# The order in which 64 experts' weights are streamed: rank bits reversed, or largest and smallest in turn

## The chip, the cores and the metric

One core of a Trainium2 chip runs the whole program in one launch. The metric is device time in microseconds (us). The core has engines that run side by side and meet at semaphores: TensorE (PE, matrix products; PEld is its weight load), VectorE (DVE), ScalarE (ACT), GpSimd (POOL) and SyncE (SP), which here does nothing but issue DMAs and wait. Transfers from HBM run on 16 DMA engines that all queues share.

## The reference

Two transformer blocks over 512 tokens of width 1024, all in float32. The part that matters is the mixture of experts (MoE) of the first block: a router picks 8 of 64 experts for each token, and each chosen expert adds its result, weighted by a gate.

```
scores = sigmoid(h @ router_w);  e_idx = 8 best experts of each token (in 4 of 8 groups)
gate   = scores[e_idx] / sum * 2.5
expert e, for each of its tokens:  (silu(x @ w_gate[e]) * (x @ w_up[e])) @ w_down[e]
routed = sum over a token's 8 experts of gate * result;   shared expert added
```

`w_gate` and `w_up` are 1024 x 256 for each expert and `w_down` is 256 x 1024: 1 MiB each, 3 MiB an expert, 192 MiB in all. Which expert is worked on first makes no difference to the result: each of the 4096 (token, expert) results goes to a row of its own in HBM (`y_rows`), and is added up later.

## The kernel before, in words

**Tiles and turns.** An expert's tokens are cut into tiles of 64 rows (`HALF`); an expert has at least one tile, so a nearly empty one costs as much as a full tile. Two tiles make a turn: tile A (the even one) fills the upper half of the rows of TensorE's products, tile B (the odd one) the lower half, and both halves run at once, each with its own expert's weights. For tile A TensorE reads the weights where the DMA put them; for tile B VectorE first copies them (`copy_gu` at line 3223, `copy_down` at line 3234), since the two may be the same expert's.

**The order of a turn on TensorE** (lines 1478 to 1534): `turn_gu(n)` (lines 1493 and 1494: gate and up products), `turn_h(n-1)` (line 1502: transposes), `turn_rows(n+1)` (line 1480: transposes of the gathered tokens), `turn_down(n-1)` (lines 1514 and 1515), and on to `turn_gu(n+1)`. VectorE's order is `copy_gu(n)`, `turn_h(n-1)`, `copy_down(n-1)`, `copy_gu(n+1)`; there are two buffers for the copy of gate and up, so `copy_gu(n)` may begin once `turn_gu(n-2)` is done, and one for down. ScalarE does a tanh (line 2269) right after each `turn_gu`, and takes the result out of PSUM (line 2279) right after each `turn_down`. GpSimd gathers the tokens of coming turns by an indirect DMA and puts results away by another.

**The ring.** The weights of `RING = 4` experts are on the chip at a time. The experts are numbered by slot, 0 to 63, in the order in which they are loaded and worked on; slot k lies in place k mod 4. Slots 0 to 3 are always experts 0 to 3, since they are loaded before the router has spoken. The other 60 are ranked by their number of tokens on the chip, and `load_order()` says which rank (4 is the largest of the 60, 63 the smallest) goes to which slot: `counting_rows()` writes it into a constant, and line 3125 compares each expert's rank with it. Nothing is computed that depends on it but the table of slots, and with it tiles, turns and rows.

**The loads** are issued by SyncE in one fixed sequence, slot by slot (lines 744 to 757 and 789 to 799). For slot k:

```
wait until turn_gu and copy_gu are done with slot k-4       # ahead moe_g, moe_cg
issue w_gate, w_up of slot k                                # line 745
wait until gate and up of slot k-1 have landed; signal it   # landed_gu, line 752
wait until turn_down and copy_down are done with slot k-5   # ahead moe_y, moe_cd, in next_down
issue w_down of slot k-1                                    # line 748
wait until down of slot k-2 has landed; signal it           # landed_down, line 756
```

So the signal that gate and up of slot k-1 are there is given only behind the issue of slot k's gate and up, and that stands behind the issue of slot k-2's down. VectorE's `copy_gu` waits for the signal of its tile B's expert (`gu_loaded`), and TensorE's `turn_gu` waits for VectorE's copy, not for the signal itself. SyncE's waits on TensorE count whole turns: a slot whose last tile is tile t is let go when turn t // 2 is done.

**Idle turns.** The table is made for 128 tiles; the tiles that no expert needs stand at the front and are skipped four at a time.

Of the kernel before, what the change touches and what calls it, by code (L numbers as in the profile page):

```python
# [41 lines left out]
N_EXPERTS = 64  # L42
# [8 lines left out]
RING = 4  # L51
# [44 lines left out]

def load_order():

    pace = [r for r in (int(f"{n:06b}"[::-1], 2) for n in range(N_EXPERTS)) if r < N_EXPERTS - RING]
    return list(range(RING)) + [RING + r for r in pace]  # L100


def counting_rows():

    tokens = np.arange(P)[:, None] + P * np.arange(TT)[None, :]
    counts = np.broadcast_to(np.arange(P + 1)[None, :], (P, P + 1))
    pairs = (PER_TOKEN * tokens[:, :, None] + np.arange(PER_TOKEN)[None, None, :] + 1).reshape(P, -1)
    e = np.arange(P)
    prior = np.where(e < RING, (RING - e) * float(1 << 18), -e.astype(np.float64))
    order = np.concatenate([load_order(), np.zeros(P - N_EXPERTS)])  # L110
    experts = np.broadcast_to(e[None, :N_EXPERTS], (P, N_EXPERTS))
    return np.concatenate([tokens, counts, pairs, np.broadcast_to(prior[None, :N_EXPERTS], (P, N_EXPERTS)),
                           prior[:, None], order[:, None], experts], axis=1).astype(np.float32)
# [3539 lines left out]
```

How the kernel before makes its waits and increments, by code:

```python
    def wait(self):  # L220
        self.eng.wait_ge(self.sem, self.base + self.k)
# [439 lines left out]
        def ahead(eng, name, value):  # L661
            eng.wait_ge(sem(name), value + AHEAD[name])
# [25 lines left out]
        @block.sync  # L690
# [3 lines left out]
            def fill(name, u, turn, *parts):  # L694
                s = ring.slot(name, u)
                sp.wait_ge(used[s], ring.free(name, u, turn))
                for dst, src in parts:
                    sp.dma_start(dst, src).then_inc(landed[s], 16)
# [19 lines left out]
            with sp.Fori(0, 4) as i:  # L719
                for u in range(2):
                    fill("merge", 2 * u, i,
                         (unit("merge", 2 * u, 0, KD, P), w_in[:, :, bass.ds(i * 256 + (GA0 + u * P), P)]),
                         (unit("merge", 2 * u, 1024, KD, P), w_in[:, :, bass.ds(i * 256 + (GB0 + u * P), P)]),
                         (unit("merge", 2 * u, 2048, KD, P), w_sc_out[:, :, bass.ds(i * 256 + u * P, P)]))
                    fill("merge", 2 * u + 1, i,
                         (unit("merge", 2 * u + 1, 0, 16, P), w_ssd_out[:, :, bass.ds(i * 256 + u * P, P)]))
            for u in range(2):
                if u == 1:
                    sp.wait_ge(sem("ada_sum"), ADA_MERGE["sum"] + 8 * ADA_N - 1)
                fill("w_o", u, 0, (unit("w_o", u, 0, KD, 512), w_o[:, :, 512 * u:512 * u + 512]))
            sp.wait_ge(sem("ada_sum"), ADA_MERGE["sum"] + 8 * ADA_N)
# [17 lines left out]
            def landed_gu(slot, nth):  # L750
                sp.wait_ge(sem(f"ring_in{slot}"), nth * 32)
                sp.sem_inc(sem("gu_loaded"), 1)
```

## Time and profile before

| | us |
|---|---|
| three runs | 3205.16, 3205.81, 3209.31 |
| median | 3205.81 |
| the profiled execution | 3207.94 |
| its span | 3206.3 |
| TensorE busy | 3067.1 (96%) |
| VectorE busy | 1856.3 (58%) |
| the turns of the experts | about 1062 to 1704 |

The span is cut by the profile from the first to the last instruction; all positions below are us from its start. Over the whole span the 16 DMA engines move 177 GB/s on average; in the slices of the experts it is 364 to 392 GB/s. The busy time of TensorE overlaps the waits of its own pipeline, so it is not TensorE at its peak.

### The profile page before, as it was taken

Reading aid. Unit: us, or ns where it says so; the run is one execution under the profiler, and the core shown is the slowest. Engines: PE = TensorE matmul, PEld = TensorE weight load, DVE = VectorE, ACT = ScalarE, POOL = GpSimd, SP = SyncE. Lnnn points to the kernel's source line nnn. Section 1 sums busy time; section 2 is a strip of 40 time slices with the busy share of each in tenths; the row PEclk is TensorE's granted clock in tenths of the full one; section 3 lists DMA queues with packets and bytes.
Section 4 is the critical chain, followed back from the end, with each engine's and each line's share of the span. In section 5 each row is a group of like instructions: output and inputs, shape, how many; then the busy total and the mean of one; then the engine's idle time right before and its main releaser. Section 6 shows DMA issues by size and latency. Waiting matters only on the chain. (4 is left out here: it accounts for less than half of the span.)

```text
span 3206.3 us, 39693 instructions
## 1 busy us (share of the span) xinstructions
PE 3067.1 (96%) x12422; PEld 1759.3 (55%) x12423; DVE 1856.3 (58%) x3939; ACT 561.1 (18%) x1282; POOL 243.5 (8%) x377
## 2 busy tenths in 40 slices
PE   7999999999999899999997998999999899899998
PEld 4765666644447333333333445488744687488643
DVE  6767676565446534434334387565667555465667
ACT  1002222210002122222221216310000233100000
POOL 1000000011100222222212000000000000000000
PEclk9999999999999899999999999999999999899999
DMA  7673132388753479999997231022344324022342
GB/s 228 188 221 100 59 99 66 112 274 275 237 182 132 181 311 388 379 381 376 392 364 284 105 105 34 33 99 79 131 165 143 99 80 138 26 99 79 131 184 105
DMA packets 270691, 566.55 MB, mean 177 GB/s; under 512 B 27017, under 2 KB 162804, under 8 KB 245994
## 3 DMA queue, kind: packets, MB, share of 16 engines
q1 hardware_dynamic: 213712, 413.72, 36.2%
q0 software_dynamic: 46992, 140.43, 12.5%
q10 hardware_dynamic: 9866, 10.82, 1.0%
q8 instruction: 71, 1.16, 0.1%
q14 instruction: 50, 0.41, 0.0%
HBM read 554.22 MB, written 36.83 MB: 184 GB/s over the span
## 5 line engine op out<-in xcount | busy, mean ns | idle before, releaser
L1493 PE MATMUL ps<-WR,hT 128*64 x832 | 374.4, 604 | 20.7 <-issue 20.7
L1494 PE MATMUL ps<-WR,hT 128*64 128x512 f32 x832 | 374.4, 604 | 0.0
L1937 PE MATMUL ps<-WR 128*128 128x512 f32 x784 | 337.4, 592 | 1.0 <-DVEq L3511 0.7
L1493 PEld LDWEIGHTS ps<-WR,hT 128*64 128x64 f32 x832 | 115.5, 140 | 264.3 <-issue 264.2
L1937 PEld LDWEIGHTS ps<-WR 128*128 128x128 f32 x784 | 148.6, 190 | 188.9 <-issue 186.0
L3223 DVE COPY WR<-WR 128x1024 f32 x208 | 130.8, 691 | 161.8 <-SPq L752 108.6
L1157 PE MATMUL ps<-hT,WR 128*128 128x512 f32 x512 | 223.8, 593 | 0.6 <-DVE WR L2752 0.6
L1896 PE MATMUL ps<-WR 128*128 128x256 f32 x960 | 217.0, 379 | 0.0
L1896 PEld LDWEIGHTS ps<-WR 128*128 128x128 f32 x960 | 182.4, 190 | 24.8
L1514 PE MATMUL ps<-WR 128*64 x416 | 189.5, 598 | 2.7 <-DVEq L3236 1.8
L1515 PE MATMUL ps<-WR 128*64 128x512 f32 x416 | 189.6, 598 | 0.0
L1340 PE MATMUL ps<-WR 128*128 128x512 f32 x384 | 168.7, 598 | 1.5 <-ACT WR L2433 0.8
L3557 DVE TENSOR_TENSOR WR<-ps,WR 128x256 f32<-128x256 f32 x210 | 86.0, 423 | 145.1 <-PE ps L1896 143.3
L1896 PE MATMUL ps<-hT,WR 128*128 128x256 f32 x720 | 165.2, 379 | 0.0
L1157 PEld LDWEIGHTS ps<-hT,WR 128*128 128x128 f32 x512 | 96.5, 190 | 112.7 <-issue 111.0
L3234 DVE COPY WR<-WR 128x1024 f32 x104 | 67.3, 690 | 142.8 <-PE ps L1515 122.9
L1896 PEld LDWEIGHTS ps<-hT,WR 128*128 128x128 f32 x720 | 136.6, 190 | 18.5
L2581 DVE SCALAR_TENSOR_TENSOR WR<-xr,csil,WR 128x512 f32<-128x512 f32 x168 | 126.3, 752 | 11.7 <-DMA xr<-in_ada_w 3.3
L1340 PEld LDWEIGHTS ps<-WR 128*128 128x128 f32 x384 | 72.7, 192 | 91.0 <-issue 88.7
L1494 PEld LDWEIGHTS ps<-WR,hT 128*64 128x64 f32 x832 | 115.5, 140 | 0.0
L1173 PE MATMUL ps<-WR,hT 128*128 128x256 f32 x512 | 112.8, 379 | 0.0
L1234 PE MATMUL ps<-hT,WR 128*128 128x512 f32 x256 | 112.0, 594 | 0.0
(475 smaller groups left out, 4712.8 us busy)
## 6 DMA issues: line engine op xcount, KB each, us to landing
WR<-in_w_gate SPq DMA_DIRECT2D x64, 1024.0 KB
WR<-in_w_up SPq DMA_DIRECT2D x64, 1024.0 KB
WR<-in_w_down SPq DMA_DIRECT2D x64, 1024.0 KB
WR<-in_mlp_w SPq DMA_DIRECT2D x56, 1024.0 KB, 6.2
WR<-in_mlp_w SPq DMA_DIRECT2D x20, 2048.0 KB, 7.5
xr<-in_ada_w POOLq DMA_DIRECT2D x32, 1024.0 KB, 5.5
WR<-in_w_in SPq DMA_DIRECT2D x56, 512.0 KB, 6.9
xr<-in_w_ada POOLq DMA_DIRECT2D x16, 1024.0 KB, 5.4
```

The lines of the kernel that those rows point to most:

```text
L1157: last = mm(ps[:, k % 2, :], w[:, kk, k * P:(k + 1) * P], hT[:, kk, :], start=(kk == 0), stop=(kk == KD - 1))
L1173: last = mm(ps[:, h, (t % 2) * GW:(t % 2 + 1) * GW], hT[:, kk, t * P:(t + 1) * P], w[:, kk, :], start=(kk == 0), stop=(kk == KD - 1))
L1234: last = mm(ps[:, MERGE_BANKS[u][n], :], w[:, k, :], rhs[:, k, :], start=(k == 0), stop=(k == KD - 1))
L1340: last = mm(ps[:, 2 * t + u, :], src[:, k, t * P:(t + 1) * P], w[:, k, :], start=(k == 0), stop=(k == KD - 1))
L1493: mm(out[0:HALF], xT[u][:, k, 0:HALF], wa[:, :, k, :], start=(k == 0), stop=(k == KD - 1))
L1494: last = mm(out[HALF:P], xT[u][:, k, HALF:P], wb[:, :, k, :], start=(k == 0), stop=(k == KD - 1))
L1514: mm(ps[0:HALF, 5 + n, :], heT[u][:, f, 0:HALF], wa[:, f, n, :], start=(f == 0), stop=(f == FE - 1))
L1515: last = mm(ps[HALF:P, 5 + n, :], heT[u][:, f, HALF:P], wb[:, f, n, :], start=(f == 0), stop=(f == FE - 1))
L1896: last = mm(ps[:, bank, 0:2 * P], weights[:, k, :], tokens[:, k, :], start=(k == 0), stop=(k == 3))
L1937: return mm(ps[:, bank, :], rows, weights, start=(row == 0), stop=(row == PAST[phase] - 1))
L2581: ins = V.scalar_tensor_tensor(dst, w[:, k - lo, :], c[:, k:k + 1], dst, ALU.mult, ALU.add)
L3223: last = V.tensor_copy(gu_b[u][:, D * n:D * (n + 1)], w[:, D * n:D * (n + 1)])
```

## The change

One line of `load_order()`. Slots 0 to 3 stay. The 60 ranks that follow were in the order of their six bits reversed, with those of 60 and over left out; they now come as the first, the last, the second, the last but one and so on.

```diff
-    pace = [r for r in (int(f"{n:06b}"[::-1], 2) for n in range(N_EXPERTS)) if r < N_EXPERTS - RING]
+    pace = [r for n in range((N_EXPERTS - RING) // 2) for r in (n, N_EXPERTS - RING - 1 - n)]
     return list(range(RING)) + [RING + r for r in pace]
```

Both lists hold each of 0 to 59 once. The router of the reference, run on the inputs, gives these token counts: experts 0 to 3 have 20, 49, 91 and 16 tokens, the largest of the others has 332, then 184, 183, 180, 164, 151, 136 and 129, and so on down to 2. That makes 102 tiles: one expert with 6, seven with 3, nineteen with 2 (expert 2 among them) and thirty-seven with 1. By slot, beginning with slot 0, the tiles are

```
before  1 1 2 1 | 6 1 2 1 2 1 2 1 3 1 2 1 2 1 1 3 1 2 1 2 1 1 1 3 1 2 1 2 1 1
                  3 1 2 1 2 1 2 1 3 1 2 1 2 1 1 3 1 2 1 2 1 1 1 3 1 2 1 2 1 1
after   1 1 2 1 | 6 1 3 1 3 1 3 1 3 1 3 1 3 1 3 1 2 1 2 1 2 1 2 1 2 1 2 1 2 1
                  2 1 2 1 2 1 2 1 2 1 2 1 2 1 2 1 2 1 2 1 2 1 1 1 1 1 1 1 1 1
```

(30 slots to a line behind the bar.) With two empty tiles at the front the tiles are numbered 0 to 103, in turns 0 to 51, in both kernels; slot 0 is tile 2.

## Rows read from the trace of the kernel before

**Rows 1.** Stretches of the turns: busy us (count) by engine, TensorE clock, DMA share, GB/s.

```profile
1144.00:1284.00 140.00, 139.97 (x696) 53.62 (x694) 57.47 (x96) 32.51 (x48) 32.25 (x48) 1.00 0.97 384
...
1180.00:1220.00 40.00, 39.97 (x202) 15.64 (x200) 15.92 (x27) 9.81 (x15) 9.70 (x14) 1.00 1.01 410
```

**Rows 2.** Instructions by line, 1060 to 1704: count, busy us, mean ns, idle before.

```profile
L1494 PE MATMUL ps<-WR,hT 128*64 128x512 f32 x832 | 374.4, 604 | 0.0
...
L1515 PE MATMUL ps<-WR 128*64 128x512 f32 x416 | 189.6, 598 | 0.0
```

**Rows 3.** TensorE's waits, 1060 to 1704: us in total, times, longest.

```profile
PE ps L1493 <- issue: 20.7, 6, 6.2
```

**Rows 4.** ScalarE in order of time: start, us; one tanh ends each turn's gate product.

```profile
1310.45 0.38 ACT L2269 ACTIVATE WR<-ps 128x256 f32<-128x256 f32 x1
1322.23 0.38 ACT L2269 ACTIVATE WR<-ps 128x256 f32<-128x256 f32 x1
1338.16 0.38 ACT L2269 ACTIVATE WR<-ps 128x256 f32<-128x256 f32 x1
...
1373.38 0.38 ACT L2269 ACTIVATE WR<-ps 128x256 f32<-128x256 f32 x1
1385.44 0.38 ACT L2269 ACTIVATE WR<-ps 128x256 f32<-128x256 f32 x1
1397.22 0.38 ACT L2269 ACTIVATE WR<-ps 128x256 f32<-128x256 f32 x1
1415.35 0.38 ACT L2269 ACTIVATE WR<-ps 128x256 f32<-128x256 f32 x1
...
1544.44 0.38 ACT L2269 ACTIVATE WR<-ps 128x256 f32<-128x256 f32 x1
1558.16 0.38 ACT L2269 ACTIVATE WR<-ps 128x256 f32<-128x256 f32 x1
...
1616.86 0.38 ACT L2269 ACTIVATE WR<-ps 128x256 f32<-128x256 f32 x1
1635.10 0.38 ACT L2269 ACTIVATE WR<-ps 128x256 f32<-128x256 f32 x1
```

**Rows 5.** SyncE in order of time: gate loads of slots 24, 28, 29, 36 and 63.

```profile
1292.27 0.33 SPq L745 DMA_DIRECT2D WR<-in_w_gate  x1
...
1331.46 0.33 SPq L745 DMA_DIRECT2D WR<-in_w_gate  x1
...
1344.83 0.33 SPq L745 DMA_DIRECT2D WR<-in_w_gate  x1
...
1405.99 0.33 SPq L745 DMA_DIRECT2D WR<-in_w_gate  x1
...
1670.55 0.34 SPq L745 DMA_DIRECT2D WR<-in_w_gate  x1
```

**Rows 6.** VectorE, then TensorE, at the wait of turn 46, in order of time.

```profile
1622.77 2.70 DVE L3223 COPY WR<-WR 128x1024 f32 x4 [11.83 <-SPq L752]
...
1625.94 1.11 PE L1493 MATMUL ps<-WR,hT 128*64 x1 [4.96 <-issue]
```

**Rows 7.** ScalarE, SyncE and VectorE from the end of one down product on.

```profile
1639.39 1.02 ACT L2279 ACTIVATE lngb<-ps 128x1024 f32<-128x1024 f32 x1 [2.68 <-PE ps L1515]
...
1639.54 0.33 SPq L748 DMA_DIRECT2D WR<-in_w_down  x1
1642.07 0.33 SPq L745 DMA_DIRECT2D WR<-in_w_gate  x1
1642.50 0.38 SPq L745 DMA_DIRECT2D WR<-in_w_up  x1
...
1644.27 2.50 DVE L3223 COPY WR<-WR 128x1024 f32 x4 [2.69 <-SPq L752]
```

**Rows 8.** Two more: a short stretch behind a wait, and GpSimd's DMA queue (packets, MB, share), 1060 to 1700.

```profile
1405.00:1414.00 9.00, 9.00 (x30) 2.77 (x32) 4.57 (x8) 0.00 (x0) 0.34 (x1) 0.70 1.00 411
...
q0 software_dynamic: 14688, 32.68, 13.3%
```

## The prediction

> **What bounds the kernel now.** I began with the busy shares by stretch, since the diff touches only the expert turns. There TensorE is busy without a gap (139.97 of 140 us) while the DMA engines are at 0.97, and at 1.01 with 410 GB/s in the densest part [rows 1]. Two limits lie side by side, so I worked out both. The group of instructions by line has 832 gate-and-up products and 416 down products [rows 2]: at 16 and 8 a turn, 52 turns for the 104 tiles. The tanh behind each gate product gives the period: 1310.45 to 1322.23 is 11.78, and the turns alternate with 11.67 [rows 4], so 11.72 a turn, 5.86 us a tile. That is TensorE's demand. The loads' demand I read from SyncE: slots 29 to 36 are issued 61.16 us apart, 8.74 each, and slots 28 to 36 74.53 apart, 9.32 each [rows 5]; both hold the rows of tokens that share the engines (32.68 MB in 640 us [rows 8]). So an expert costs about 9.03 us of loading, and an expert of one tile brings TensorE 5.86 us of work, one of two 11.7. Over all 60 loaded ones it is even; locally a run of small experts starves TensorE.
>
> The waits say the same. TensorE waits 20.7 us ahead of gate products, in 6 pieces [rows 3]. By the tanhs, five turns are too long: turn 22 by 4.21 (15.93 less 11.72), 26 by 0.34, 28 by 6.41, 40 by 2.00, 46 by 6.52, together 19.5 us [rows 4]. Tile B of turns 22, 28, 40 and 46 is tile 45, 57, 81 and 93; in the slot table each lies in or right behind a run of two or three experts of one tile (slots 24 to 26, 32 and 33, 47 and 48, 54 to 56). So the time that the order can give back is 19.5 us, and no more. Part of it is clock: turn 46 waited 4.96 us [rows 6] and was late by 6.52, so 1.6 us came behind the wait; a stretch behind the wait of turn 28 has a granted clock of 0.70 of 2.4 GHz, so it stood at 1.2 GHz for part of it [rows 8].
>
> **The change, part by part.** The tiles, the turns and the instructions are the same in number: 102 tiles, 104 with the empty ones. What moves is which expert is in which slot. Whatever lies ahead of turn 0 and behind turn 51 is untouched.
>
> *A, the waits that go: -19.5 us.* Up to slot 54 the new order has no two experts of one tile next to each other but slots 0 and 1, which are loaded long before. From slot 20 on two experts bring three tiles.
>
> *B, the loads that start later.* The big experts now come first: slots 4 to 19 hold 35 tiles, 2.2 an expert, 12.8 us of TensorE's time against 9.03 of loading. There the ring is full and SyncE waits. Slot 24 can be loaded only when slot 20 is let go; it ends at tile 43, so with the gate product of turn 21, whose tanh is at 1322.23 [rows 4]; before, that load went out at 1292.27 [rows 5]. The loads are 31 us behind by then, and I priced what that costs. Slots 24 to 54 are 31 experts with 47 tiles, 275.4 us of TensorE; their loading takes 270.9 us at 8.74 and 288.9 at 9.32. So the stretch is late by 0 to 13.5 us, 4.5 at 9.03. The copy for a turn is usually ready some 4 us ahead of its product (copy and product of rows 6 and 7: a copy of 2.5 us begun at 1644.27 for a turn that follows the tanh of 1646.87), so the first 4 cost nothing. Averages flatter, though: before they are even, and yet 19.5 us are lost to lumps. So I take the upper half, 9 less the cover of 4, 5 us, and 0 to 12 as ends. Turn 48 then needs both slots 56 and 57, 18.1 us of loading in 11.7: 6.4 late, less what is left of the cover; I take 3, ends 0 and 6.
>
> The Trainium skill, in "DMA: Bandwidth & Descriptors", section "Bandwidth", gives 425 GB/s for a core's large loads alone. At that rate an expert's 3.15 MB and the 0.5 MB of token rows beside it would take an estimated 8.5 us, under the 8.9 that TensorE has for it here, and the 5 us would be nothing; the trace reaches 410 over 40 us, so it nearly agrees.
>
> *C, the block at the end: +22.5 us.* This is the term that decides. Slots 55 to 63 are nine experts of one tile each: slot 55 is tile 95 (turn 47's B), and turns 48, 49, 50, 51 take slots 56 and 57, 58 and 59, 60 and 61, 62 and 63. Follow SyncE for turn 50. Its B is slot 61; the signal that 61 has landed comes behind the issue of slot 62, that behind the issue of slot 60's down, and that waits until slot 56's down is free: slot 56 is tile 96, in turn 48, so until the down product of turn 48 ends. But on TensorE that product stands directly ahead of the gate product of turn 50. So the copy for turn 50, which has otherwise a turn's time to spare, begins only when TensorE has nothing left to do. Turn 49 is the same (slot 58's down waits for slot 54, tile 94, turn 47), and turn 51 (slot 62's down waits for slot 58, turn 49). In turn 48 it is not so: slot 56's down waits for slot 52, turn 45. The old order never has it: with a 2 or 3 among four slots the slot waited for lies a turn further back. The price is a row for each step: the down product's end lets ScalarE start at 1639.39, down goes out at 1639.54, gate at 1642.07, up at 1642.50 until 1642.88, the signal was taken up at 1644.27 by a copy of 2.50 [rows 7]; from a copy's end (1625.47) to the product (1625.94) 0.47 [rows 6]. That is 1647.2 less 1639.3, 7.9 us. Of the 1.39 us between the last issue and the copy I estimate that half was the landing, so 7.2 at least. Three times 7.5 is 22.5; ends 21.6 and, if each landing is late by 2 as well, 30. It doesn't depend on the DMA rate. What hides it now is that the signal is a turn ahead.
>
> *D, the clock.* Each wait of this length can put TensorE to 1.2 GHz for a while. Turn 46 paid 1.6 for it; turn 28 was late by 6.41 with a wait that I put at 3.6 to 4, so 2.6; turn 22 with a wait of about 4 was late by 4.21, so nothing. I take 2.2 for each of three turns, 6.6; ends 0 and 9.
>
> The sum: -19.5 + 5 + 3 + 22.5 + 6.6 = 17.6 us. The profiled execution's 3207.94 (its span 3206.3 and 1.6 around it) would become 3225.5; it lies 2.1 above the median of the three runs, 3205.81, and from that I forecast **3223 us**.
>
> **The rivals.**
>
> *The smooth order wins (faster).* If the signals in the last turns come in time, nothing is left but A and the lateness of B. Mechanism and place: `copy_gu` of turns 49 to 51; it decides by whether the signal of slots 59, 61 and 63 is given before or after the down product of two turns earlier. Then the change is -19.5 + 5, the time 3205.8 - 14.5 = 3191 us, and 3186 with B at nothing. For it: all old waits lie at runs of small experts, and these go. Against it: the sequence of SyncE is fixed, and the tiles of slots 54 to 60 are as counted. I give it 7 in 100.
>
> *The late start governs all (slower still).* If the loads after slot 24 go at the pace that they had from there to the end, 378.28 us for 39 slots or 9.70 [rows 5], the last gate load goes out at 1323.5 + 378.3 = 1701.8 in place of 1670.55, 31 us late, and the end with it: 3237 us. Against it: in 9.70 there is time in which SyncE waited for TensorE, since the ring was full at times. 15 in 100.
>
> *Only the bare block.* C at 21.6 and neither clock nor late loads: +2.1, 3208 us; with one of the two, +5. This is the case of no change that could be told: 10 in 100.
>
> *The change does nothing that counts*, as the ranks were the same or the table was read in another way: both lists hold 0 to 59 once and the comparison is with numbers, so that the tiles must move; within the case before.
>
> **How the numbers follow.** My case (+11 to +26) has 68, the late start 15, the bare block 10, the smooth order 7. The range should reach the bare block's upper half and the late start: low 3209, high 3237. What a measurement of this kernel can tell is about 0.2%, 6.4 us. Faster by more: 0.07. Within: 0.10. Slower by more: 0.83.
>
> **What would show it.** In the profile after: no long turn between turns 3 and 27; SyncE waiting for TensorE more, the gate load of slot 24 at 1323 to 1325; small late turns of 0 to 2 us every third turn from about turn 28; and at the very end three turns of about 19 to 21 us in a row, each with a copy that starts some 4 us after ScalarE's start on the last down product, the last down product ending near 1721 in place of 1704. TensorE's wait ahead of gate products would be about 30 us in place of 20.7. DMA share well under 0.97 in 1144 to 1284. If the last three turns are 11.7 us apart, C is wrong, and the time falls below 3200; if the middle turns are late by more than 12 us together, B is too small.

## The result, and the profile after

| | before | changed |
|---|---|---|
| median of 16 runs, us | 3205.54 | 3217.63 |
| lowest and highest | 3197.72, 3214.69 | 3214.32, 3223.48 |
| profiled execution, us | 3207.94 | 3215.32 |
| its span | 3206.3 | 3213.6 |

The ratio is 1.0035, with a 95% interval of 1.0028 to 1.0042: slower by 9 to 13.5 us. The forecast was 3223, +17.6 by its terms. "Late" below is what a turn's start is behind the start of the turn before it plus 11.72 us. Behind turn 51 comes one more leg, from its start to the end of the last down product, 17.7 us where nothing waits; it is late by what it takes beyond that.

First the wait of TensorE ahead of the gate products, in the page of the changed kernel (busy us, mean ns, idle before). It was 20.7 [rows 3] and is 29.7. Without the waits ahead of turns 1 and 2, which come long and short with either order (last section), it was 14.5 and is 25.9.

```profile
L1493 PE MATMUL ps<-WR,hT 128*64 x832 | 376.4, 606 | 29.7 <-issue 17.5
```

Next the stretches of the changed kernel (columns as in [rows 1]). From 1144 to 1564 TensorE has no gap but for 0.2 us in all, and the loads show the late start and the catching up: DMA share 0.84 in 1144 to 1284, where it was 0.97, and 1.01 with 407 GB/s in 1424 to 1564. Nearly all that is lost lies in the last stretch, with the clock at 0.91.

```profile
1144.00:1284.00 140.00, 139.97 (x694) 53.59 (x692) 57.45 (x96) 31.93 (x48) 32.26 (x48) 1.00 0.84 326
1284.00:1424.00 140.00, 139.77 (x694) 53.43 (x692) 57.75 (x96) 32.06 (x48) 32.44 (x48) 1.00 0.98 392
1424.00:1564.00 140.00, 139.97 (x696) 53.73 (x694) 56.47 (x94) 32.51 (x48) 32.89 (x48) 1.00 1.01 407
1564.00:1713.00 149.00, 120.29 (x541) 42.66 (x535) 44.29 (x74) 25.00 (x38) 21.71 (x33) 0.91 0.83 323
```

ScalarE in order of time, changed kernel: the tanhs of turns 46 to 51, and behind two of them the copy-out (L2279) that follows a down product. They answer to [rows 4] and the first of [rows 7]. The tanhs are 11.77, 18.38, 21.61, 20.72 and 19.16 us apart.

```profile
1610.89 0.38 ACT L2269 ACTIVATE WR<-ps 128x256 f32<-128x256 f32 x1
...
1622.66 0.38 ACT L2269 ACTIVATE WR<-ps 128x256 f32<-128x256 f32 x1
...
1641.04 0.38 ACT L2269 ACTIVATE WR<-ps 128x256 f32<-128x256 f32 x1
...
1662.65 0.38 ACT L2269 ACTIVATE WR<-ps 128x256 f32<-128x256 f32 x1
1666.92 1.02 ACT L2279 ACTIVATE grow<-ps 128x1024 f32<-128x1024 f32 x1 [2.74 <-PE ps L1515]
1683.37 0.38 ACT L2269 ACTIVATE WR<-ps 128x256 f32<-128x256 f32 x1
...
1702.53 0.38 ACT L2269 ACTIVATE WR<-ps 128x256 f32<-128x256 f32 x1
...
1712.64 1.02 ACT L2279 ACTIVATE lngb<-ps 128x1024 f32<-128x1024 f32 x1 [4.51 <-PE ps L1515]
```

The chain ahead of turn 50, read across SyncE, VectorE and TensorE of the same kernel. Turn 48's down product ends (ScalarE starts at 1666.92), only then does slot 60's down go out (1667.07), behind it slot 62's gate and up, and behind these the signal for slot 61, whose gate load had gone out at 1654.13. The copy starts at 1671.22, the product at 1674.19 after 7.42 us of nothing. Turn 49's chain is the same with 7.88 us.

```profile
1654.13 0.33 SPq L745 DMA_DIRECT2D WR<-in_w_gate  x1
1654.57 0.39 SPq L745 DMA_DIRECT2D WR<-in_w_up  x1
1667.07 0.33 SPq L748 DMA_DIRECT2D WR<-in_w_down  x1
1669.21 0.33 SPq L745 DMA_DIRECT2D WR<-in_w_gate  x1
1669.64 0.38 SPq L745 DMA_DIRECT2D WR<-in_w_up  x1
```

```profile
1671.22 2.50 DVE L3223 COPY WR<-WR 128x1024 f32 x4 [15.65 <-SPq L752]
```

```profile
1653.06 1.11 PE L1493 MATMUL ps<-WR,hT 128*64 x1 [7.88 <-DVEq L3226]
...
1674.19 1.11 PE L1493 MATMUL ps<-WR,hT 128*64 x1 [7.42 <-issue]
...
1691.88 1.11 PE L1493 MATMUL ps<-WR,hT 128*64 x1 [4.37 <-DVEq L3226]
```

The bytes of slot 61 were not what turn 50 waited for. In the 4 us in which TensorE ran out of work the DMA engines were nearly idle, at 0.10 and 41 GB/s (columns as in [rows 1]): what had been asked for had landed, and only the signal was missing.

```profile
1664.00:1668.00 4.00, 2.77 (x14) 0.74 (x10) 0.00 (x0) 1.21 (x2) 0.00 (x0) 1.00 0.10 41
```

### The profile page after: what moved, and what is told of

Same layout as the page of the kernel before. It is cut to its first block and busy times, and to the rows that moved or that the text cites. A ratio compares the mean times of both kernels' runs of the same rounds, so it can differ in the third digit from the quotient of the medians.

```text
span 3213.6 us, 39693 instructions
## 1 busy us (share of the span) xinstructions
PE 3064.7 (95%) x12422; PEld 1756.3 (55%) x12423; DVE 1855.8 (58%) x3939; ACT 561.0 (17%) x1282; POOL 246.0 (8%) x377
## 3 DMA queue, kind: packets, MB, share of 16 engines
q1 hardware_dynamic: 213712, 413.72, 36.2%
q0 software_dynamic: 46992, 140.43, 12.5%
## 5 line engine op out<-in xcount | busy, mean ns | idle before, releaser
L1493 PE MATMUL ps<-WR,hT 128*64 x832 | 376.4, 606 | 29.7 <-issue 17.5
L2581 DVE SCALAR_TENSOR_TENSOR WR<-xr,csil,WR 128x512 f32<-128x512 f32 x168 | 126.3, 752 | 12.1 <-DMA xr<-in_ada_w 4.1
```

The lines of the kernel that those rows point to most:

```text
L1493: mm(out[0:HALF], xT[u][:, k, 0:HALF], wa[:, :, k, :], start=(k == 0), stop=(k == KD - 1))
L2581: ins = V.scalar_tensor_tensor(dst, w[:, k - lo, :], c[:, k:k + 1], dst, ALU.mult, ALU.add)
```

## The experiments

**The kernel before, once more.** No edit.

> The kernel before, once more against itself. Ratio 1.000 within 0.002 by every theory. What it is for is the trace: the profile of before had five long turns (22, 26, 28, 40, 46; 19.5 us) and lost another 6 us between the first two gate products, where the changed kernel lost 2.4. If the waits at runs of small experts come from the order, they stand at the same turns again and make 17 to 23 us. If the opening wait is chance, it is another length here; if it belongs to the old order, it is again about 6 us.

Ratio 1.000 (0.999 to 1.0009). In its trace TensorE's waits ahead of gate products are

```profile
PE ps L1493 <- issue: 17.7, 6, 5.4
```

and ScalarE's tanhs show the long turns 22 and 46 where they were:

```profile
1314.46 0.38 ACT L2269 ACTIVATE WR<-ps 128x256 f32<-128x256 f32 x1
1331.68 0.38 ACT L2269 ACTIVATE WR<-ps 128x256 f32<-128x256 f32 x1
...
1608.36 0.38 ACT L2269 ACTIVATE WR<-ps 128x256 f32<-128x256 f32 x1
1627.88 0.38 ACT L2269 ACTIVATE WR<-ps 128x256 f32<-128x256 f32 x1
```

Turns 22, 28, 40 and 46 are late again; 26 is not. In all 20.2 us where [rows 4] have 19.5 (19.7 by the products' starts). So the waits belong to the order. The opening wait between the first two gate products was 6.2 us in the first profile and is 3.0 here.

**The changed kernel, once more.** No edit.

> The changed kernel once more. Ratio to before 1.003 to 1.0055. The block at the end predicts that turns 49, 50 and 51 begin 17 to 23 us after the turn before, each by a copy that follows the end of a down product by 4 to 5 us, and 33 to 38 us lost over all turns; chance would show other turns. The opening wait tells, with the kernel before, whether it goes with the order.

Ratio 1.0035 (1.0021 to 1.0049). Turns 48 to 51 are late by 4.9, 10.2, 9.1 and 7.6, with 1.7 behind them and 1.7 in turns 28 and 46: 35.2 us, where the first trace of this kernel has 36.2. The opening wait is long here (turns 1 and 2 late by 6.2 together), where it was short in the first trace (1.1). It comes in both lengths with both orders, so it is chance and not the order's; it is worth some 5 us.

**The big ones first, without the run at the end.**

```diff
-    pace = [r for n in range((N_EXPERTS - RING) // 2) for r in (n, N_EXPERTS - RING - 1 - n)]
+    big, mid, small = list(range(8)), list(range(8, 26)), list(range(N_EXPERTS - RING - 1, 25, -1))
+    pace = [r for b in big for r in (b, small.pop(0), small.pop(0))]
+    pace += [r for m in mid for r in (m, small.pop(0))]
```

> The changed order with one thing undone: the run of nine one-tile experts at the end is gone. The eight big ones still come first, each now followed by two small ones, and then eighteen of two tiles, each followed by one small; the last two slots are a 2 and a 1. Theory (the run at the end costs about 29 us, the late start of the loads about 7): no turn longer than 15 us from turn 44 on, small waits of 0 to 3 us every third turn in the last 20 turns, in all 5 to 15 us lost, and a ratio to before of 0.997 to 1.001. Rival (the loads that start late rule): the loads are late in the same way as in the changed kernel, so its ratio stays at 1.003 or above.

Ratio 0.9972 (0.9962 to 0.9982), median 3196.98: faster than both kernels. Turns 7, 12, 17 and 22 are late by 1.3 each, 38 to 50 by 1.0 to 1.7 every third turn, and none by more: 12.5 us in all. So the run of nine was what made the changed order slow, and the rival is out.

One condition of this expectation did not hold: the loads are late here too, but by less than half. Slot 28's gate load goes out 284.1 us behind the start of turn 0, where the kernel before has 269.4 and the changed one, in its second trace, 302.4 (all three with a long opening wait). What the full lateness costs is to be read from the changed kernel's own traces: up to turn 47 its turns are late by 3.2 and 1.7 us in all.

**The middle ones first.**

```diff
+    pace = [r for m in mid for r in (m, small.pop(0))]
+    pace += [r for b in big for r in (b, small.pop(0), small.pop(0))]
```

(with `big`, `mid` and `small` as above)

> The other way round: eighteen of two tiles first, each followed by a small one, and then the eight big ones, each followed by two small ones. No run of more than two one-tile experts, and each run of two stands behind an expert of three or more tiles. Theory (waits come from runs of small experts, and a late start of loads costs a little): nearly all of the 19.5 us of before come back, 3 to 9 us lost in all, ratio 0.9955 to 0.9985. Rival (the loads' own rate sets the stage and the order only moves the waits about): ratio 1.000 with 15 us or more of waits somewhere.

Ratio 0.9954 (0.9941 to 0.9967), median 3190.35, 14 us under the kernel before (3204.62) and 25 under the changed one (3215.44) in their repeats: this is the version that beats both. TensorE's waits (6.8 us holds the opening wait of 2.4) and a stretch of it, same columns as above:

```profile
PE ps L1495 <- issue: 6.8, 5, 2.4
...
PE ps L1495 <- DVEq L3228: 2.0, 2, 1.0
```

```profile
1144.00:1284.00 140.00, 139.89 (x692) 53.44 (x690) 58.21 (x96) 32.53 (x48) 33.21 (x48) 1.00 1.00 400
```

6.6 us late in all from turn 3 on, where 3 to 9 were expected (the ratio lies just below the expected 0.9955), and the clock stands at 2.4 GHz through all the turns from there on. The loads run at share 1.00 and 400 GB/s from the start, in place of 0.97 before and 0.84 in the changed kernel. The order explains this, though no run takes it apart: with pairs of a two-tile and a one-tile expert first, the ring has free places at once, and the big experts at the end need no lead.

**The changed order with fewer bytes in the last slots.**

```diff
-                    sp.dma_start(ring_at(slot, 2048 * n, 2048), src[e]).then_inc(sem(f"ring_in{slot}"), 16)
+                    sp.dma_start(ring_at(slot, 2048 * n, n_cols), src[e][:, 0:n_cols]).then_inc(
+                        sem(f"ring_in{slot}"), 16)
```

(Shortened: `n_cols` is 512 for slots 58 to 63 and 2048 for the others, `load_down` is changed in the same way, and the last two rounds of the loop are written out for it)

> The changed order; of slots 58 to 63 only the first quarter of each weight's columns is loaded (the rest of the place keeps old weights, so the result leaves them out). SyncE's sequence is the same. Theory (the signal of a landed expert stands behind a down load that waits for a product): turns 49, 50 and 51 are late as before, 6 to 11 us each, 24 to 31 us with the last leg, since no byte is waited for; ratio to before 1.002 to 1.005. Rival (two experts cannot be loaded in one turn, the DMA rate is the limit): with a quarter of the bytes turns 49 to 51 are 11.7 to 13 us apart and the ratio is 0.996 to 0.999.

Ratio 1.0038 (1.0024 to 1.0052). A stretch of its end, and ScalarE's tanhs of turns 48 to 51:

```profile
1642.00:1714.00 72.00, 50.06 (x214) 17.12 (x210) 16.79 (x28) 10.08 (x16) 6.71 (x10) 0.86 0.30 92
```

```profile
1643.41 0.38 ACT L2309 ACTIVATE WR<-ps 128x256 f32<-128x256 f32 x1
1664.82 0.38 ACT L2309 ACTIVATE WR<-ps 128x256 f32<-128x256 f32 x1
1685.43 0.38 ACT L2309 ACTIVATE WR<-ps 128x256 f32<-128x256 f32 x1
1704.62 0.38 ACT L2309 ACTIVATE WR<-ps 128x256 f32<-128x256 f32 x1
```

The DMA engines are at 0.30 and 92 GB/s, and yet the turns are 21.4, 20.6 and 19.2 us apart, as in the changed kernel. With the last leg turns 49 to 51 are late by 28.6 us. TensorE doesn't wait for bytes there. Had I tried this alone, the sequence of SyncE would look like the only cause.

**The changed order with the signal ahead of the wait.**

```diff
-                    landed_gu((r - 1) % RING, i + (1 if r else 0))
+                    if not (k >= 60 and k % 2 == 0):
+                        landed_gu((r - 1) % RING, i + (1 if r else 0))
+                    if k >= 59 and k % 2:
+                        landed_gu(r, i + 1)
                     next_down((r - 1) % RING, expert_of(i * RING + (r - 1)), turns_a, turns_b)
```

(Shortened: the last two rounds of the loop are written out for it, k is the slot, and the `landed_gu` of slot 63 behind the loop is dropped)

> The changed order, all weights loaded; for slots 59, 61 and 63 SyncE waits for gate and up to land and gives the signal before it waits for the place of the down load ahead. So the block is taken away and the DMA rate stays. Theory with the block alone: turns 49 to 51 are late by under 2 us each, ratio 0.997 to 0.999. Theory with both limits close together (a turn needs 18.1 us of loading, and each load now goes out alone): still late by 5 to 9 us each, ratio 1.001 to 1.004. I hold the second for likelier, 2 to 1.

Ratio 1.0033 (1.0018 to 1.0048). Its tanhs of turns 48 to 51:

```profile
1637.25 0.38 ACT L2308 ACTIVATE WR<-ps 128x256 f32<-128x256 f32 x1
1654.71 0.38 ACT L2308 ACTIVATE WR<-ps 128x256 f32<-128x256 f32 x1
1674.87 0.38 ACT L2308 ACTIVATE WR<-ps 128x256 f32<-128x256 f32 x1
1694.60 0.38 ACT L2308 ACTIVATE WR<-ps 128x256 f32<-128x256 f32 x1
```

17.5, 20.2 and 19.7 us apart. In this trace 28.9 us are late in all where the changed kernel has 36.2 and 35.2; most of the gain is in turn 49. The ratio can't tell the two kernels apart. With all bytes to be moved, two experts a turn are late with or without the blocked signal.

This is not the rate of the DMA engines alone, though. The edit gives the signal earlier, but the gate and up loads of slots 60 and 61 still stand behind slot 58's down, and that behind turn 47's down product. And it adds a wait: SyncE has to see slot 59 land before it issues slot 58's down, and slot 61 before slot 60's. Each time this wait ended last. Turn 48's down product ended at 1659.0 and slot 60's down went out at 1662.76, and meanwhile the DMA engines ran dry, here at 0.44 (columns as above) and again at 0.35 in 1680 to 1684.

```profile
1660.00:1664.00 4.00, 0.00 (x0) 0.00 (x0) 1.67 (x3) 0.01 (x1) 1.18 (x2) 0.77 0.44 152
```

How much of the lateness is rate, and how much the place at which the loads may begin and the added wait, no run here separates.

**Both at once.** The two edits together.

> Both at once: a quarter of the bytes for slots 58 to 63, and the signal ahead of the wait for the down place. If block and loading are the two causes and no third, turns 49 to 51 are late by less than 5 us in all, 8 to 14 us are lost over all turns, and the ratio is 0.996 to 0.999. A third cause (the copies, the clock, the gather of tokens) would leave 5 us or more a turn.

Ratio 0.9974 (0.9964 to 0.9984). The same four tanhs:

```profile
1641.95 0.38 ACT L2308 ACTIVATE WR<-ps 128x256 f32<-128x256 f32 x1
1653.74 0.38 ACT L2308 ACTIVATE WR<-ps 128x256 f32<-128x256 f32 x1
1668.62 0.38 ACT L2308 ACTIVATE WR<-ps 128x256 f32<-128x256 f32 x1
1680.61 0.38 ACT L2308 ACTIVATE WR<-ps 128x256 f32<-128x256 f32 x1
```

11.8, 14.9 and 12.0 us apart: 4.6 us late in turns 49 to 51 and 9.3 in all. So there are two limits of nearly one height at the end, the blocked signal and the loading of two experts from the place where it begins, and no third that is worth more than these 4.6 us. Taking either away alone shows the other.

**The changed order from its end.**

```diff
+    pace = [r for n in range((N_EXPERTS - RING) // 2) for r in (n, N_EXPERTS - RING - 1 - n)][::-1]
```

> The changed order of the 60 ranks read from its end: the nine one-tile experts stand at slots 4 to 12, the biggest at slot 63. If what a run costs does not hang on where it stands, four or five turns from turn 4 on are late by 4 to 9 us each, 27 to 38 us together with the clock, and small waits of 0 to 2 us every third turn follow; ratio 1.004 to 1.008. If it costs only at the end, where no later turn can make it good (the late start of the loads), those turns are late but the ratio stays under 1.002.

Ratio 1.0084 (1.0061 to 1.0106) from four runs, median 3232.38, a little above what I gave. The tanhs of turns 3 to 7:

```profile
1111.29 0.38 ACT L2269 ACTIVATE WR<-ps 128x256 f32<-128x256 f32 x1
1131.71 0.38 ACT L2269 ACTIVATE WR<-ps 128x256 f32<-128x256 f32 x1
1153.14 0.38 ACT L2269 ACTIVATE WR<-ps 128x256 f32<-128x256 f32 x1
1174.11 0.38 ACT L2269 ACTIVATE WR<-ps 128x256 f32<-128x256 f32 x1
1196.65 0.38 ACT L2269 ACTIVATE WR<-ps 128x256 f32<-128x256 f32 x1
```

Four turns of 20.4 to 22.5 us, and 10.7 us more in turns 8 to 10: 46.7 us in all, where I had expected 27 to 38. A run of small experts costs wherever it stands, and that it costs only at the end is out. It is one of ten here, since slot 3 has one tile too, and more turns need two new experts each; I take this for the reason of the surplus, but no run shows it.

## Why the prediction was right, point by point

**The sum.** By the profiles, late turns went from 19.7 to 36.2 us, and in the second pair from 20.2 to 35.2: +16.5 and +15. The forecast was +17.6. The medians moved by 12.1 and 10.8. What lies between I can name in part. The two first profiles differ by only 7.3 us of span, and three things that the forecast has no term for make the difference. Turn 0 began at 1062.09 in the one before and at 1059.25 in the one after, 2.8 us earlier. The opening wait was long in the one before (turns 1 and 2 late by 6.1 together) and short in the one after (1.1). And the part behind the turns was shorter with the changed order: 1501.2 and 1500.5 us against 1502.6 and 1503.5. By the first two of these, above all, the last down product ended at 1712.5 and not near 1721. Of the part behind the turns a stretch of 100 us shows how, in the changed kernel and the one before:

```profile
1725.00:1825.00 100.00, 89.31 (x270) 46.54 (x270) 55.85 (x98) 19.86 (x43) 20.18 (x38) 0.92 0.72 264
```

```profile
1716.00:1816.00 100.00, 90.11 (x267) 47.63 (x268) 55.86 (x98) 19.37 (x42) 20.22 (x38) 0.89 0.71 264
```

The granted clock there is 0.92 against 0.89, and 0.88 over 104 us in the repeat of the kernel before, with the same work. Whether the order has a part in it I haven't tested, but the traces point that way: the three whose last turns wait for the blocked signal (the changed kernel twice and the one with fewer bytes) have 1500.5 to 1501.4 us behind the turns, the seven others 1502.3 to 1504.6. 16 less 2 leaves 14 against a measured 9 to 13.5; the rest stays open. Two traces a kernel don't fix how often the opening wait is long.

**A, the waits that go (-19.5).** Right: turns 22, 26 and 40 are on time, turn 28 is late by 0.4 and 46 by 2.4 (both counted under B), and the repeat of the kernel before shows that its waits are no chance.

**B, the late start (+8 with turn 48).** The size was right, 3.2 us in turns 28, 43 and 46 where I took 5, and 3.9 in turn 48 where I took 3. A late turn every third from turn 28 on, as I had listed among the signs, did not show. And one number in it was wrong. I put slot 24's gate load about 1 us behind turn 21's tanh. SyncE, ScalarE (tanh of turn 21, then the copy-out behind turn 20's down product) in the changed kernel:

```profile
1318.89 0.33 SPq L748 DMA_DIRECT2D WR<-in_w_down  x1
1321.43 0.35 SPq L745 DMA_DIRECT2D WR<-in_w_gate  x1
```

```profile
1314.47 0.38 ACT L2269 ACTIVATE WR<-ps 128x256 f32<-128x256 f32 x1
1318.74 1.02 ACT L2279 ACTIVATE grow<-ps 128x1024 f32<-128x1024 f32 x1 [2.73 <-PE ps L1515]
```

It went out 7.0 us behind the tanh, because slot 22's down stood ahead of it and waited for turn 20's down product. This is the block of term C again, which the prediction has only at the end; here it hides. That the lateness still came out small is due to the pace: slots 24 to 54 are issued 264.35 us apart (1321.43 to 1585.78), 8.81 each, where I took 9.03, and TensorE has 8.9. Nor are the two limits even over all 60 loaded experts, as the prediction has it: their 97 tiles give TensorE 9.5 us an expert by its own figures, against 9.03 of loading, so that late loads can catch up. The estimate at 425 GB/s comes to 8.6 us by its own figures and not to 8.5, which changes nothing.

**C, the block (+22.5).** The mechanism is right and confirmed by the chain of rows above. TensorE waited 7.88, 7.42 and 4.37 us, 19.7 in all. The third was shorter than my price: slot 62's down needs only turn 49's product, which ended at 1687.5, and behind it no gate and up have to be issued before the signal for slot 63. The prediction priced the last turn like the others, though its sequence is another. What it says of the DMA rate was half wrong: "It doesn't depend on the DMA rate" holds where fewer bytes have to come (DMA share 0.30, no gain), but with the signal freed and all bytes to be moved the last turns are late by nearly as much. The two limits were set against each other as rivals in the experiments, and are twins in the kernel.

**D, the clock (+6.6).** Turns 49 to 51 and the leg behind are late by 10.8, 9.4, 6.0 and 2.9, together 29.1; less the waits that is 9.4 us for the clock, just over the upper end of 9 that I gave. The granted clock over the last 73 us is 0.86 in the changed kernel, and 1.00 in the last 68 before; it fell to 1.2 GHz in each of the four waits ahead of turns 48 to 51. The price of one fall was right, 2.4 us where I took 2.2. The number was not: there were four and not three, since turn 48's wait of 3.72 us, which I had under B, put the clock down too, and turn 49 paid for it. The trace bears the price out: behind the four waits the products ran 5.6, 3.5, 2.9 and 5.7 us at 1.2 GHz, and half of that, the estimated loss, is about 9 us.

```profile
1640.00:1713.00 73.00, 50.39 (x213) 17.28 (x211) 16.79 (x28) 10.43 (x17) 6.72 (x10) 0.86 0.65 246
```

```profile
1636.00:1704.00 68.00, 65.31 (x317) 23.93 (x313) 23.53 (x39) 14.69 (x23) 11.83 (x18) 1.00 0.70 273
```

C and D together were forecast as 29.1 and came out as 29.1; that is luck, since C was 2.8 us too high and D as much too low.

The Trainium skill, in "TensorE: Matmul & The Clock Gate", section "HAM oscillation — how this bites in real kernels", says that a kernel whose products wait for data falls back to the slow clock again and again and pays for it beyond the wait. By that rule, the trace agrees: 9.4 us on top of 19.7.

**The rivals.** The smooth order that wins is not this one, but it exists: it is what the two spread orders show, at 0.9972 and 0.9954, once the run is gone. The late start that governs all has the last gate load go out 31 us late. Counted from the start of turn 0, in pairs of traces with the same opening wait, it was 10 and 11 us late (618.3 for 608.5, and 614.9 for 603.9), and the spread order with the big ones first, whose loads are late by less than half as much, was fast. The bare block is out by the 7.1 us of B and the 9.4 of the clock.

## What to carry to other kernels

When a queue issues in one fixed order, write down for each signal what stands ahead of it and what that waits for, in units of the consumer's steps; a signal that ends up behind the consumer's own previous step costs a full hand-over each time (here 7.4 to 7.9 us, and as much with a quarter of the bytes). Order pieces of uneven work so that no stretch as long as the ring needs loads faster than they come. Largest and smallest in turn leaves the surplus of small ones in one run; here both orders that spread it were faster. And where removing one suspected limit changes nothing, remove the other as well before concluding: two limits of one height hide each other.

## What was not expected of the hardware

Ahead of the second gate product TensorE stands still for either 2.4 to 3.0 or 6.2 to 6.7 us with nothing to wait for in the profile. Of ten traces of these programs five have the one and five the other, and both orders have both. What makes the wait long stays open. The longer one also brings a slower product behind it (9.5 to 9.8 us for 7.1), and that is the clock: in all five it falls to 1.2 GHz within the long wait, and in none of the others (granted clock 0.66 over 1073 to 1083 before, 1.00 in the changed kernel). And the clock's drops behind the turns fall otherwise from one trace to another, and with them a part of 1500 us moves by up to 4 us (1500.5 to 1504.6) although its instructions are the same.
